# Two feed-forwards of a two-block network: a tile's two weight products as seven products of quarters (Strassen's scheme, Winograd's form)

## The chip, the cores and the metric

One core of one Trainium2 chip runs the whole program in one launch. The metric is the device time of that launch in microseconds (us); lower is better. The kernel before takes 3156.23 us, the median of 3 runs (3155.23 to 3160.46).

## What is computed

512 tokens of width 1024 go through two blocks of two layers each. Every layer is a mixer and a feed-forward behind an RMS norm. The change touches the feed-forwards of the second block alone:

```python
def swiglu(h, w_gate, w_up, w_down):
    return (jax.nn.silu(h @ w_gate) * (h @ w_up)) @ w_down

def second_block(x, ...):
    for l in range(DEPTH):              # DEPTH = 2
        ...
        h = rmsnorm(x, norm_ffn[l])
        x = x + swiglu(h, ffn_w_gate[l], ffn_w_up[l], ffn_w_down[l])
    return x
```

The gate and up weights are 1024 x 2816, the down weights 2816 x 1024, all float32.

## The kernel before

Activations are kept transposed: `h(k)`, k from 0 to 7, holds 128 channels by 512 tokens. Each float32 operand of TensorE is split into a rounded part and its rest (type fp32r), and each product takes three matmuls (`mm3`, line 481): high by high, low by high, high by low. The normed input lies in `xhi` and `xlo` (the list `X8`).

**Weights** (class `Weights`, line 287). A unit of up to 2048 columns is loaded by SyncE into one of three raw buffers (`wraw`), rounded by ScalarE into one of two `whi` (`round`), and VectorE takes the rest into `wlo` (`rest`). `round` of a unit waits until TensorE is done with the unit two before; a load waits for the `rest` of the unit three before. The programs of ScalarE and VectorE call `round` and `rest` with the unit that is being used, and do the next one.

**A feed-forward stage** (`ffn`, line 1095; stages `swiglu0` and `swiglu1`) has 22 tiles of 128 hidden channels. A tile's unit holds 128 columns of gate (named u) and 128 of up (named g) for all 8 input blocks. TensorE makes each with 8 x 3 matmuls of 512 tokens. ScalarE applies SiLU out of PSUM, VectorE multiplies by g, ScalarE rounds the product (`hid.hi`), VectorE takes the rest (`hid.lo`). The down product runs by groups of 8, 8 and 6 tiles, each group a group of tiles later than its ups; its units are 256 columns wide (two output blocks), and VectorE adds each output block from PSUM to `hT` (line 212).

**The start of a stage** (class `Fresh`, line 718). Tile 0 multiplies the not yet normed input (times the gain), so that TensorE doesn't wait for the norm; its results are scaled by `rs` afterwards. Meanwhile ScalarE makes `rs`, and VectorE and ScalarE make the normed, split input block by block; tile 1 takes the blocks as they come. In the midst of this (`midway`) comes the unit of tile 2.

**The end of a stage** (class `Carry`, line 680). After each output block is added to `hT`, ScalarE rounds it and squares it, VectorE takes its rest, and GpSimd (POOL) adds up the squares of blocks 1 to 6. The next stage's first tile needs the sum of squares before its third input block (`norm.sum`, at k == 2).

Apart from these sums of squares (78 additions of 128 x 512) GpSimd has almost no arithmetic. The engines wait for each other with semaphores that count; each engine's order is that in which its program is written.

## Time and profile before

| | before |
|---|---|
| median of 3 runs | 3156.23 us (3155.23 to 3160.46) |
| the profiled execution's own time | 3158.57 us |
| its span, first to last instruction | 3156.8 us |
| mean granted TensorE clock | 0.99 |
| TensorE matmul / weight load busy | 97% / 77% |
| VectorE / ScalarE / GpSimd busy | 50% / 37% / 4% |
| matmuls | 16544 |

The page of the profile gives each engine's busy time as a share of the span; a busy matmul row is not an engine at its peak, since matmuls overlap and their ends are modelled. So the time from one matmul's start to the next says more than the length of one. `swiglu0` runs from about 2003 to 2373 us, `swiglu1` from about 2784 to 3147 us.

### The profile page before, as it was taken

To read this page: it belongs to the slowest core of one execution; us is meant where nothing else is said; L and a number is where in the kernel's file an instruction comes from. 1 tells how busy PE (TensorE), PEld (TensorE's weight loads), DVE (VectorE), ACT (ScalarE), POOL (GpSimd) and SP (SyncE) were. 2 spreads that over 40 slices of the span, in tenths; PEclk is the share of its full clock that TensorE was granted. 3 is DMA by queue.
4 is the path that set the end of the run, shared out by engine and by line. 5 is a ranking of instruction groups with operands and counts; after the bars stand their busy time and mean duration, and the time that the engine had idled before them with its cause. 6 is when DMAs were issued, how large, how long until landed. Compare 5 with 4: busy or idle time off the path is not lost.

```text
span 3156.8 us, 38539 instructions
## 1 busy us (share of the span) xinstructions
PE 3047.3 (97%) x16544; PEld 2433.2 (77%) x16544; DVE 1571.3 (50%) x1919; ACT 1178.3 (37%) x1533; POOL 142.0 (4%) x154
## 2 busy tenths in 40 slices
PE   8999888999999999999999998999999999999999
PEld 6897676778887767778887775688888888788887
DVE  6444455655544765465444655533336454553333
ACT  5433332543322564443323545422224433342221
POOL 1010000100000100000001100000000000000000
PEclk9999999999999999999999999999999999999999
DMA  4362000223332311223332330233323222233331
GB/s 156 110 202 63 15 29 28 101 73 94 94 87 90 102 67 54 94 72 102 100 94 77 91 87 27 58 102 93 94 94 104 84 84 84 80 94 94 96 100 59
DMA packets 350490, 270.51 MB, mean 86 GB/s; under 512 B 28672, under 2 KB 331264, under 8 KB 350064
## 3 DMA queue, kind: packets, MB, share of 16 engines
q1 hardware_dynamic: 346384, 252.83, 26.8%
q0 software_dynamic: 3936, 15.22, 1.4%
q8 instruction: 130, 2.13, 0.3%
q14 instruction: 40, 0.33, 0.0%
HBM read 261.73 MB, written 6.29 MB: 85 GB/s over the span
## 4 chain that ended last, share of the span: by engine, by line
PE 86%; DVE 7%; ACT 5%; issue 1%; POOL 0%; DMA 0%; DVEq 0%; SPq 0%; ACTq 0%; POOLq 0%
PE ps L189 85%; ACT arena L203 2%; ACT whi L206 1%; DVE arena L212 1%; DVE arena L220 1%; DVE wlo L212 1%; DVE hT L212 1%; PE ps L192 1%; DVE xlo L220 1%; ACT L203 0%; DVE sml L229 0%; POOL arena L212 0%; DVE xlo L212 0%; ACT arena L206 0%; DVE split L212 0%
## 5 line engine op out<-in xcount | busy, mean ns | idle before, releaser
L189 PE MATMUL ps<-xhi,whi 128*128 128x512 f32 (+2 forms) x2176 | 866.1, 398 | 17.1 <-DVE xlo L212 5.6
L189 PE MATMUL ps<-split,whi 128*128 128x512 f32 (+2 forms) x2640 | 832.7, 392 | 22.2 <-DVE split L212 11.3
L189 PE MATMUL ps<-xlo,whi 128*128 128x512 f32 (+2 forms) x2176 | 849.5, 390 | 0.0
L189 PE MATMUL ps<-xhi,wlo 128*128 128x512 f32 (+2 forms) x2176 | 849.4, 390 | 0.0
L212 DVE TENSOR_TENSOR wlo<-wraw,whi 128x2048 fp32r<-128x2048 f32 (+4 forms) x258 | 550.6, 2137 | 498.9 <-ACT whi L206 498.8
L189 PEld LDWEIGHTS ps<-split,whi 128*128 128x128 f32 (+1 forms) x2640 | 490.5, 189 | 153.5 <-issue 30.2
L206 ACT ACTIVATE whi<-wraw 128x2048 fp32r<-128x2048 f32 (+4 forms) x258 | 456.1, 1771 | 362.0 <-PE ps L189 352.0
L189 PE MATMUL ps<-split,wlo 128*128 128x512 f32 (+2 forms) x1320 | 510.0, 386 | 0.0
L189 PEld LDWEIGHTS ps<-xhi,whi 128*128 128x128 f32 (+2 forms) x2176 | 408.3, 188 | 122.2 <-issue 15.0
L189 PEld LDWEIGHTS ps<-xhi,wlo 128*128 128x128 f32 (+2 forms) x2176 | 408.5, 188 | 88.0 <-issue 5.1
L189 PEld LDWEIGHTS ps<-xlo,whi 128*128 128x128 f32 (+2 forms) x2176 | 408.2, 188 | 88.3
L189 PE MATMUL ps<-arena 64*64 64x64 f32 (+8 forms) x4118 | 297.5, 262 | 24.6 <-ACT arena L203 9.9
L212 DVE TENSOR_TENSOR hT<-hT,ps 128x512 f32<-128x512 f32 x216 | 148.3, 686 | 322.7 <-PE ps L189 317.7
L206 ACT ACTIVATE arena<-ps 128x512 f32<-128x512 f32 (+2 forms) x262 | 144.4, 563 | 401.0 <-PE ps L189 311.7
L189 PEld LDWEIGHTS ps<-arena 64*64 64x64 f32 (+4 forms) x4118 | 213.2, 145 | 103.6 <-issue 54.0
L189 PEld LDWEIGHTS ps<-split,wlo 128*128 128x128 f32 (+1 forms) x1320 | 249.6, 189 | 53.9 <-issue 4.0
L212 DVE TENSOR_TENSOR arena<-arena,ps 128x512 f32<-128x512 f32 (+5 forms) x160 | 103.6, 647 | 368.0 <-PE ps L189 359.1
L206 ACT ACTIVATE split<-arena 128x512 fp32r<-128x512 f32 (+1 forms) x161 | 98.3, 615 | 430.0 <-DVE arena L212 421.0
L212 POOL TENSOR_TENSOR arena<-arena 128x512 f32<-128x512 f32 x78 | 106.8, 1373 | 2437.6 <-ACT arena L203 2436.7
L203 ACT ACTIVATE arena<-ps 128x512 f32<-128x512 f32 (+4 forms) x133 | 76.8, 584 | 262.7 <-PE ps L189 253.4
L203 ACT ACTIVATE arena<-arena 128x512 f32<-128x512 f32 (+4 forms) x154 | 93.4, 622 | 160.2 <-DVE arena L220 123.0
L212 DVE TENSOR_TENSOR split<-arena,split 128x512 fp32r<-128x512 f32 (+1 forms) x161 | 107.0, 670 | 80.6 <-ACT split L206 78.4
(115 smaller groups left out, 1924.3 us busy)
## 6 DMA issues: line engine op xcount, KB each, us to landing
wraw<-in_ffn_w_up SPq DMA_DIRECT2D x128, 512.0 KB, 5.2
wraw<-in_ffn_w_down SPq DMA_DIRECT2D x32, 1024.0 KB, 5.1
wraw<-in_odd_w_in SPq DMA_DIRECT2D x24, 1024.0 KB, 5.2
wraw<-in_ffn_w_gate SPq DMA_DIRECT2D x44, 512.0 KB, 4.0
wraw<-in_xattn_wkv SPq DMA_DIRECT2D x16, 1024.0 KB, 5.4
wraw<-in_xattn_wq SPq DMA_DIRECT2D x8, 1024.0 KB, 5.3
wraw<-in_xattn_wo SPq DMA_DIRECT2D x8, 1024.0 KB, 5.3
wraw<-in_cd_w_in SPq DMA_DIRECT2D x8, 1024.0 KB, 5.4
```

The lines of the kernel that those rows point to most:

```text
L189: return self.e.matmul(out, lhsT, rhs, start=start, stop=stop, skip_group_check=True)
L192: return self.e.transpose(out, in_, ident)
L203: return self.e.activation(out, in_, f, bias=bias, scale=scale, accum_out=acc)
L206: return self.e.activation(out, in_, ACT.Copy, scale=scale)
L212: return self.e.tensor_tensor(out, a, b, op)
L220: return self.e.scalar_tensor_tensor(out=out, in0=a, scalar=s, in1=b, op0=op0, op1=op1)
```

## The change

The stages `swiglu0` and `swiglu1` are made by a new function, `folded`. Tiles 0 to 2 are computed as before. From tile 3 on, a tile's weights are four quarters (A11, A12 are gate, A21, A22 are up; the second figure is the half of the input channels), the input is four quarters as well (B11 to B22, by halves of channels and of tokens), and both outputs come from seven products of quarters instead of eight. A product has 4 x 3 matmuls of 256 tokens.

- GpSimd makes four sums of weight quarters per tile (S1, S2, S4, and S3 in the place of A21 in the raw buffer). ScalarE rounds, and VectorE takes the rest of, 1536 columns more per tile; ScalarE waits for all four sums before it rounds the unit.
- VectorE makes four sums of input quarters (T1 to T4) once per stage, 1024 elements per partition each, and their rests; ScalarE rounds them.
- Bank a takes P1; ScalarE copies it out, and P6 and P7 are added up in the same bank, with a copy between. Bank c takes P5, and P3 on top. VectorE adds four halves of 256 tokens from PSUM to ScalarE's copies. SiLU then reads SBUF. A tile is multiplied, rounded and split in the next tile's turn (`finish(n - 1)`).
- The down groups are 3, 3, 3, 3, 3, 3 and 4 tiles; their units are 512 columns wide (4 output blocks), 14 units in place of 12, 56 additions to `hT` per stage in place of 24. In the last group the first unit runs over all 4 blocks at once, input tile by input tile (`by_tiles`).
- `FreshKept` keeps the normed input in full for T1 to T4.

The core of the diff:

```diff
+            if n in self.folded:
+                sums, hi, _, maker, tile = self.folded[n]
+                act.wait_ge(maker.of("sums", tile))
+                act.copy(final[1], final[0]).then_inc(*self.made_hi.up("quarters", n))
+                act.copy(hi, sums).then_inc(*self.made_hi.up(n))
+            else:
+                act.copy(final[1], final[0]).then_inc(*self.made_hi.up(n))
...
-            dve.wait_ge(self.made_hi.of(n))
+            dve.wait_ge(self.made_hi.of("quarters", n) if n in self.folded else self.made_hi.of(n))
             *first, final = self.halves(n)
             for raw, hi, lo in first:
                 dve.tt(lo, raw, hi.bitcast(F32), ALU.subtract)
-            dve.tt(final[2], final[0], final[1].bitcast(F32), ALU.subtract).then_inc(*self.made_lo.up(n))
+            if n in self.folded:
+                dve.tt(final[2], final[0], final[1].bitcast(F32), ALU.subtract)
+                sums, hi, lo, _, _ = self.folded[n]
+                dve.wait_ge(self.made_hi.of(n))
+                dve.tt(lo, sums, hi.bitcast(F32), ALU.subtract).then_inc(*self.made_lo.up(n))
+            else:
+                dve.tt(final[2], final[0], final[1].bitcast(F32), ALU.subtract).then_inc(*self.made_lo.up(n))
...
+        def folded(stage, w_u, w_g, w_down, ends, prev, nxt):
+            S = Stage(stage, sem)
+            nt, H = 22, 256
...
+            FIRST = 3
...
+            def group_of(n):
+                return min(n // 3, 6)
+            groups = [[n for n in range(nt) if group_of(n) == i] for i in range(7)]
...
+            def order():
+                for i, g in enumerate(groups):
+                    for n in g[0:3]:
+                        yield "up", n
+                    if i:
+                        yield "down", i - 1
+                yield "up", 21
+                yield "down", 6
...
+            def fold(n):
+                m = W.number[W.stage, ("up", n)]
+                W.folded[m] = (sums[m % 2], *extra(m % NSPL), S.G, n)
+                return m
+            def tensor(pe):
+                def product(b, u, e, a, x, first, *event, unit=None):
+                    for k in range(4):
+                        if a in ("s1", "s2", "s4"):
+                            i = ("s1", "s2", "s4").index(a)
+                            hi, lo = (t[:, i * T + k * P:i * T + k * P + P] for t in e)
+                        else:
+                            kk, c = {"a11": (k, 0), "a12": (4 + k, 0), "s3": (k, P), "a22": (4 + k, P)}[a]
+                            hi, lo = u.hi[:, kk, c:c + P], u.lo[:, kk, c:c + P]
+                        s = operand(x, k)
+                        pe.mm(b[:, 0:H], hi, s.hi, first and k == 0, False)
+                        pe.mm(b[:, 0:H], lo, s.hi, False, False)
+                        i_ = pe.mm(b[:, 0:H], hi, s.lo, False, k == 3)
+                    i_.then_inc(*up(S.P, *event, unit=unit))
+                def seven(n):
+                    u = W.take(("up", n), *unit(n))
+                    e = extra(fold(n) % NSPL)
+                    a, b, c, d = (ps.take(name, n) for name in "abcd")
+                    pe.wait_ge(W.ready(("up", n)), ps.empty("a", n), norm.made(7))
+                    product(a, u, e, "a11", "b11", True, "p1", n)
+                    pe.wait_ge(ps.empty("b", n))
+                    product(b, u, e, "a12", "b21", True, "p2", n)
+                    pe.wait_ge(ps.empty("c", n), S.V.of("t1"))
+                    product(c, u, e, "s1", "t1", True, "p5", n)
+                    pe.wait_ge(ps.empty("d", n), S.V.of("t4"))
+                    product(d, u, e, "a22", "t4", True, "p4", n)
+                    pe.wait_ge(S.A.of("p1", n), S.V.of("t2"))
+                    product(a, u, e, "s2", "t2", False, "u2", n)
+                    pe.wait_ge(S.A.of("p5", n))
+                    product(c, u, e, "s4", "b22", False, "c12", n)
+                    pe.wait_ge(S.A.of("u2", n), S.V.of("t3"))
+                    product(a, u, e, "s3", "t3", False, "u3", n, unit=("up", n))
...
+                        g = groups[n]
+                        for _ in add_tensor(pe, S, downs[n], [hid[k % 6] if k < 18 else hid[k - 18] for k in g],
+                                            [P] * len(g), lambda k: S.V.of("hid_lo", g[k]), by_tiles=n == 6):
...
+            def vector(dve):
...
+                    if n >= FIRST:
+                        finish(n - 1)
+                        for name, dst, half in (("b", y, slice(0, H)), ("c", y, slice(H, T)), ("d", g, slice(0, H)),
+                                                ("a", g, slice(H, T))):
+                            made = {"b": "p2", "c": "c12", "d": "p4", "a": "u3"}[name]
+                            kept_ = {"b": "p1", "c": "u2", "d": "u3", "a": "p5"}[name]
+                            dve.wait_ge(S.P.of(made, n), S.A.of(kept_, n))
+                            dve.tt(dst[:, half], dst[:, half], ps.ap(name, n)[:, 0:H], ALU.add).then_inc(
+                                *up(S.V, name, n, frees=(name, n)))
+                        dve.wait_ge(S.A.of("silu", n), S.V.own())
+                        dve.tt(y, y, g, ALU.mult).then_inc(*up(S.V, "hid", n))
+                        return
...
+                def finish(n):
+                    d = place(n)
+                    dve.wait_ge(S.A.of("hid_hi", n), S.V.own())
+                    dve.tt(d.lo, tb[n % 2], d.hi.bitcast(F32), ALU.subtract).then_inc(*up(S.V, "hid_lo", n))
+                dve.wait_ge(S.V.own())
+                dve.tt(tq["t1"][0], B12, B11, ALU.subtract).then_inc(*up(S.V, "t1", "sum"))
+                dve.wait_ge(S.V.own())
+                dve.tt(tq["t2"][0], B22, tq["t1"][0], ALU.subtract).then_inc(*up(S.V, "t2", "sum"))
+                dve.wait_ge(S.V.own())
+                dve.tt(tq["t4"][0], B21, tq["t2"][0], ALU.subtract).then_inc(*up(S.V, "t4", "sum"))
+                for what, n in order():
+                    if what == "up":
+                        up_tile(n)
+                        if n == 0:
+                            dve.wait_ge(S.V.own())
+                            dve.tt(tq["t3"][0], B22, B12, ALU.subtract).then_inc(*up(S.V, "t3", "sum"))
+                            low("t1")
+                            low("t2")
+                            low("t4")
+                        if n == 1:
+                            low("t3")
+                    else:
+                        if n == 6:
...
+                        for name, _, _, blocks in downs[n]:
+                            W.rest(dve, name)
+                            for key, m in blocks:
+                                d = h(key[-1])
+                                dve.wait_ge(S.P.of(*key), S.V.own())
+                                dve.tt(d, d, ps.ap(*key), ALU.add).then_inc(*up(S.V, "h", *key, frees=key))
+                                if n == 6 and carry and key[-1]:
+                                    carry.vector(dve, key[-1] - 1)
+                        if n == 6 and carry:
+                            carry.vector(dve, 7)
+            def scalar(act):
+                W.round(act, ("up", 0))
+                act.wait_ge(*ends())
+                norm.scalar(act, lambda: W.round(act, ("up", 1)))
...
+                    if n >= FIRST:
+                        for name, bank, dst, half in (("p1", "a", y, slice(0, H)), ("p5", "c", g, slice(H, T)),
+                                                      ("u2", "a", y, slice(H, T)), ("u3", "a", g, slice(0, H))):
+                            if name == "p5":
+                                finish(n - 1)
+                            if name == "u3":
+                                act.wait_ge(S.V.of("c", n))
+                                act.act(y, y, ACT.Silu).then_inc(*up(S.A, "silu", n))
+                            act.wait_ge(S.P.of(name, n), S.V.of("hid_lo", n - 2))
+                            act.copy(dst[:, half], ps.ap(bank, n)[:, 0:H]).then_inc(*up(S.A, name, n))
+                        return
...
+                for name in ("t1", "t2", "t4"):
+                    high(name)
...
+            def gpsimd(pool):
+                pool.wait_ge(*ends())
+                for n in range(FIRST, nt):
+                    m = W.number.get((W.stage, ("up", n)), 0)
+                    raw = W.raw[m % NRAW].rearrange("p (k n) -> p k n", k=8)
+                    A11, A12, A21, A22 = raw[:, 0:4, 0:P], raw[:, 4:8, 0:P], raw[:, 0:4, P:H], raw[:, 4:8, P:H]
+                    s1, s2, s4 = (sums[m % 2][:, i * T:(i + 1) * T].rearrange("p (k n) -> p k n", k=4) for i in range(3))
+                    pool.wait_ge(W.landed[m % NRAW].of(m), W.made_lo.of(m - 2))
+                    pool.tt(s1, A21, A22, ALU.add).then_inc(*up(S.G))
+                    pool.wait_ge(S.G.own())
+                    pool.tt(s2, s1, A11, ALU.subtract).then_inc(*up(S.G))
+                    pool.tt(A21, A11, A21, ALU.subtract).then_inc(*up(S.G))
+                    pool.wait_ge(S.G.own())
+                    pool.tt(s4, A12, s2, ALU.subtract).then_inc(*up(S.G, "sums", n))
...
-        then(lambda S: ffn("swiglu0", 0, 2816, D["ffn_w_gate_2"][0], D["ffn_w_up_2"][0],
-                           D["ffn_w_down_2"][0], False, S.ends, S.carry, lambda S: Carry(S, "norm_mix_2", 1)))
+        then(lambda S: folded("swiglu0", D["ffn_w_gate_2"][0], D["ffn_w_up_2"][0], D["ffn_w_down_2"][0],
+                              S.ends, S.carry, lambda S: Carry(S, "norm_mix_2", 1)))
         then(lambda S: odd(S.ends, S.carry, ("norm_ffn_2", 1)))
-        then(lambda S: ffn("swiglu1", 1, 2816, D["ffn_w_gate_2"][1], D["ffn_w_up_2"][1],
-                           D["ffn_w_down_2"][1], False, S.ends, S.carry, None))
+        then(lambda S: folded("swiglu1", D["ffn_w_gate_2"][1], D["ffn_w_up_2"][1], D["ffn_w_down_2"][1],
+                              S.ends, S.carry, None))
```

Two places of the new order. **VectorE at the start of `swiglu0`**, from the last two normed blocks' rests on (`xlo`), before the change:

```order
L212 TENSOR_TENSOR xlo<-arena,xhi 128x512 [waits swiglu0_done_vector,swiglu0_done_scalar]
L212 TENSOR_TENSOR arena<-ps2,arena 128x512 [waits swiglu0_done_tensor]
L212 TENSOR_TENSOR arena<-arena 128x512 [waits swiglu0_done_scalar]
L212 TENSOR_TENSOR arena<-arena,ps3 128x512 [waits swiglu0_done_vector,swiglu0_done_tensor]
L212 TENSOR_TENSOR split_51<-arena,split_51 128x512 [waits swiglu0_done_vector,swiglu0_done_scalar]
L212 TENSOR_TENSOR arena<-arena,ps6 128x512 [waits swiglu0_done_vector,swiglu0_done_tensor,swiglu0_done_scalar]
L212 TENSOR_TENSOR split_51<-arena,split_51 128x512 [waits swiglu0_done_vector,swiglu0_done_scalar]
L212 TENSOR_TENSOR wlo1<-wraw0,whi1 128x2048 [waits weights_hi]
```

and with the change (`split_51` is the arena in its rounded type; the rows of 1024 are T1, T2, T4, then T3, then the rests):

```order
L212 TENSOR_TENSOR arena<-arena 128x1024 [waits swiglu0_done_vector] x3
L212 TENSOR_TENSOR arena<-ps2,arena 128x512 [waits swiglu0_done_tensor]
L212 TENSOR_TENSOR arena<-arena 128x512 [waits swiglu0_done_scalar]
L212 TENSOR_TENSOR arena<-arena,ps3 128x512 [waits swiglu0_done_vector,swiglu0_done_tensor]
L212 TENSOR_TENSOR split_51<-arena,split_51 128x512 [waits swiglu0_done_vector,swiglu0_done_scalar]
L212 TENSOR_TENSOR arena<-arena 128x1024 [waits swiglu0_done_vector]
L212 TENSOR_TENSOR split_51<-arena,split_51 128x1024 x3
L212 TENSOR_TENSOR arena<-arena,ps6 128x512 [waits swiglu0_done_vector,swiglu0_done_tensor,swiglu0_done_scalar]
L212 TENSOR_TENSOR split_51<-arena,split_51 128x512 [waits swiglu0_done_vector,swiglu0_done_scalar]
L212 TENSOR_TENSOR split_51<-arena,split_51 128x1024
L212 TENSOR_TENSOR wlo1<-wraw0,whi1 128x2048 [waits weights_hi]
L212 TENSOR_TENSOR split_51<-arena,split_51 128x1536 [waits weights_hi]
```

Eight instructions of 1024 elements now stand between the normed input and the rest of tile 3's unit (`wlo1<-wraw0,whi1`), which itself has a second piece.

**ScalarE in a folded tile** (tile 4 of `swiglu0`), with the change; before, these were a rounding of 2048, a SiLU and a rounding of 512:

```order
L206 ACTIVATE whi1<-wraw2 128x2048 [waits swiglu0_done_gpsimd,weights_landed2]
L206 ACTIVATE split_51<-arena 128x1536
L206 ACTIVATE arena<-ps5 128x256 [waits swiglu0_done_tensor]
L206 ACTIVATE split_51<-arena 128x512 [waits swiglu0_done_vector]
L206 ACTIVATE arena<-ps7 128x256 [waits swiglu0_done_tensor]
L206 ACTIVATE arena<-ps5 128x256 [waits swiglu0_done_tensor]
L203 ACTIVATE arena<-arena 128x512 [waits swiglu0_done_vector]
```

The copy of P1 out of bank a (the first from `ps5`) now stands behind both roundings of the next unit and a wait for GpSimd.

## Rows read from the trace of the kernel before

**Rows 1.** The page: busy time by engine; the chain by engine.

```profile
PE 3047.3 (97%) x16544; PEld 2433.2 (77%) x16544; DVE 1571.3 (50%) x1919; ACT 1178.3 (37%) x1533; POOL 142.0 (4%) x154
PE 86%; DVE 7%; ACT 5%; issue 1%; POOL 0%; DMA 0%; DVEq 0%; SPq 0%; ACTq 0%; POOLq 0%
```

**Rows 2.** Windows: stretch, us, busy (count) of PE, PEld, DVE, ACT, POOL, clock.

```profile
2050.00:2180.00 130.00, 130.00 (x575) 107.63 (x575) 44.07 (x36) 36.17 (x36) 0.00 (x0) 1.00 0.34 97
160.00:216.00 56.00, 56.00 (x473) 56.00 (x474) 22.92 (x10) 23.54 (x28) 10.29 (x19) 1.00 0.74 230
...
2760.00:2764.00 4.00, 3.75 (x10) 2.98 (x11) 3.09 (x3) 1.04 (x2) 0.00 (x0) 0.57 0.00 0
```

**Rows 3.** Timeline of PE at 1763 us; 21 starts apart.

```profile
1763.37 0.28 PE L189 MATMUL ps<-wlo,xhi 128*128 128x256 f32 x1
...
1765.88 0.28 PE L189 MATMUL ps<-wlo,xhi 128*128 128x256 f32 x1
```

**Rows 4.** Groups by line and form: count, busy us, mean ns, idle.

```profile
L212 DVE TENSOR_TENSOR wlo<-wraw,whi 128x2048 fp32r<-128x2048 f32 x218 | 500.4, 2295 | 464.5 <-ACT whi L206 464.4
L212 DVE TENSOR_TENSOR wlo<-wraw,whi 128x1536 fp32r<-128x1536 f32 x10 | 17.6, 1758 | 11.1 <-ACT whi L206 11.1
L212 DVE TENSOR_TENSOR wlo<-wraw,whi 128x1024 fp32r<-128x1024 f32 x12 | 14.7, 1223 | 11.1 <-ACT whi L206 11.1
L212 DVE TENSOR_TENSOR arena<-arena,ps 128x256 f32<-128x256 f32 x7 | 2.9, 421 | 0.9 <-PE ps L189 0.6
...
L206 ACT ACTIVATE whi<-wraw 128x2048 fp32r<-128x2048 f32 x218 | 415.4, 1906 | 266.7 <-PE ps L189 256.7 <-DVE hT L212 10.0
L206 ACT ACTIVATE split<-arena 128x512 fp32r<-128x512 f32 x147 | 92.0, 631 | 426.8 <-DVE arena L212 418.3 <-DVE arena L220 8.5
L206 ACT ACTIVATE arena<-ps 128x256 f32<-128x256 f32 x40 | 15.3, 383 | 55.6 <-PE ps L189 38.4 <-PE ps L192 11.1 <-DMA kv_scratch<-arena 5.9
L206 ACT ACTIVATE whi<-wraw 128x1536 fp32r<-128x1536 f32 x10 | 14.8, 1483 | 51.8 <-PE ps L189 51.8
L206 ACT ACTIVATE whi<-wraw 128x1024 fp32r<-128x1024 f32 x12 | 12.6, 1048 | 5.9 <-PE ps L189 5.9
L203 ACT ACT_TABLE_LOAD x36 | 46.2, 1283 | 3.8 <-PE ps L189 3.2
```

**Rows 5.** Timeline of the start of swiglu0, DVE: start, us.

```profile
2011.38 2.29 DVE L212 TENSOR_TENSOR wlo<-wraw,whi 128x2048 fp32r<-128x2048 f32 x1 [0.79 <-ACT whi L206]
...
2023.37 2.29 DVE L212 TENSOR_TENSOR wlo<-wraw,whi 128x2048 fp32r<-128x2048 f32 x1 [2.33 <-ACT whi L206]
...
2029.01 1.48 DVE L212 TENSOR_TENSOR xlo<-arena,xhi 128x512 fp32r<-128x512 f32 x2
...
2037.99 2.29 DVE L212 TENSOR_TENSOR wlo<-wraw,whi 128x2048 fp32r<-128x2048 f32 x1 [1.11 <-ACT whi L206]
2043.75 0.69 DVE L212 TENSOR_TENSOR arena<-arena,ps 128x512 f32<-128x512 f32 x1 [3.46 <-PE ps L189]
```

**Rows 6.** Timeline of DVE and POOL at 555 us, at the end of a mixer.

```profile
555.67 1.79 DVE L220 SCALAR_TENSOR_TENSOR xlo<-hT,par,xhi 128x512 fp32r<-128x512 f32 x1
...
559.61 0.69 DVE L212 TENSOR_TENSOR hT<-hT,ps 128x512 f32<-128x512 f32 x1
...
555.62 1.29 POOL L212 TENSOR_TENSOR arena<-arena 128x512 f32<-128x512 f32 x1 [309.65 <-ACT arena L203]
...
559.62 1.30 POOL L212 TENSOR_TENSOR arena<-arena 128x512 f32<-128x512 f32 x1 [0.66 <-ACT arena L203]
```

**Rows 7.** Timeline of the start of swiglu1, DVE.

```profile
2802.77 1.48 DVE L212 TENSOR_TENSOR xlo<-arena,xhi 128x512 fp32r<-128x512 f32 x2
...
2817.52 0.69 DVE L212 TENSOR_TENSOR arena<-arena,ps 128x512 f32<-128x512 f32 x1 [3.48 <-PE ps L189]
```

**Rows 8.** Timeline of the end of swiglu0: ACT's last square, PE's sum of squares.

```profile
2374.96 0.62 ACT L203 ACTIVATE arena<-hT 128x512 f32<-128x512 f32 x1
...
2376.14 1.88 PE L189 MATMUL ps<-arena,ones 128*128 128x512 f32 x4
```

152 lines of the change are left out of this document (151 added, 1 removed).

## The prediction

> **What bounds the kernel now.** I read the page first: TensorE's matmuls are busy for 97% of the span and make up 86% of the chain that ended last, no other engine over 7% [rows 1]. So the chain is TensorE's stream, and what counts is the time from one matmul's start to the next, and every stop of that stream. The windows give the first: in swiglu0, 575 matmuls of 512 columns in 130 us, 0.226 us each; and for 256 columns, where weights or moving data lie in the arena, 473 in 56 us, 0.118 us each [rows 2]. With `xhi` and `xlo` the timeline has 21 starts of 256 columns in 2.51 us, 0.120 us each [rows 3]. All at a granted clock of 1.00, the level of 2.4 GHz. Halving the columns thus costs a little over half. The idle column of the groups says the same from the other side: VectorE waits for ScalarE's rounding and ScalarE's rounding for TensorE [rows 4].
>
> **What the seven products save.** A tile before: 48 x 0.226 = 10.85 us. A folded tile: 84 matmuls of 256; 36 of them (P1, P2, P3) move `xhi` or `xlo`, 36 x 0.120 = 4.30, and 48 lie in the arena, 48 x 0.118 = 5.68: 9.98 us. Saved 0.87 us a tile, on 19 tiles in 2 stages: **-33 us**. The down products keep their 528 matmuls of 512 per stage and cost the same.
> The Trainium skill (TensorE: Matmul & The Clock Gate, Back-to-back issue gap) says that in a stream with a weight load before each matmul the spacing is 81 ns at 128 columns and 131 ns at 512. A straight line between gives 98 ns at 256, an estimate from that page: 84 x 98 ns is 8.2 us against 48 x 131 ns, 6.3 us, so by that rule each folded tile would lose 1.9 us. The trace has 226 and 118 to 120 ns, so it speaks against the rule here.
>
> **In the middle of a stage.** I lay out one folded tile, 0 being TensorE's first matmul of it, with [rows 4]. ScalarE: copy of the last product of the tile before 0.38 (done 0.6), unit rounded 1.91 (2.5), sums rounded 1.48 (3.9), copy of P1 0.38 (4.3). TensorE wants that copy before P6, after four products, at 5.7: 1.4 us to spare. Copies of P5 (5.3, wanted at 7.2) and of bank a again (7.7, wanted at 8.6) have room too. VectorE: two halves from PSUM 0.42 each, the product 0.69 [rows 6] (2.2), rest of the unit 2.3 (4.8), rest of the sums 1.76 (6.5), wanted at 10. GpSimd: 4 x 1.30 and two waits, 5.4 us a tile, started when the rests of the unit two before are made; a whole tile of room. Per group of three tiles TensorE needs 3 x 9.98 + 72 x 0.23 = 46.5 us, VectorE about 30, ScalarE 21, GpSimd 16. The 32 more additions to `hT` per stage (0.69 us each) are in VectorE's 30 and cost nothing as long as that cover holds; without it they would cost 22 us a stage. So I put the middle at **0**. Weight loads move no more bytes and start at the same rests: 0.
>
> **The start of a stage** is where I expect the loss. Before, VectorE ends the norm at 2030.49 and has tile 3's unit split at 2040.28, 3.2 us ahead of TensorE, which ends tile 2 at about 2043.5 [rows 5]. Now between these two stand, one behind the other, because VectorE and ScalarE hand to each other: T1, T2, T4, 3 x (1.22 + 0.11 for the wait) to 34.5; u of tile 0 scaled, 35.2; ScalarE rounds T4 only to 35.6, then loads its table 1.28 and SiLU 0.63, 37.6; two products 39.1; rounding 0.63 and rest 0.69, 40.5; T3 41.8; three rests of 1.22, 45.5; tile 1's product, rounding, rest 47.6; T3's rest 48.8; ScalarE ends the second piece of tile 3's unit at 50.2; VectorE 2.29 and 1.76: **2052.8**. TensorE is free at 2043.5: a stop of 9.3 us.
> GpSimd adds to this. At 555 us a two-input VectorE instruction of 0.75 us takes 1.79 and ends 0.55 us behind the GpSimd addition that runs beside it (555.62 + 1.29 to 557.46), while the addition to `hT` from PSUM at 559.61 takes its 0.69 beside one at 559.62 [rows 6]. So a GpSimd addition and a VectorE instruction with both inputs in SBUF exclude each other, in turns, about 1.15 us for each of GpSimd's. The sums of tile 3 may start when tile 1's unit is split (2011.38 + 2.29), against the first normed blocks, which delays `midway` by 1.3 us (VectorE waits 2.33 us ahead of it now) [rows 5]; those of tile 4 when tile 2's unit is split (2025.6 before, now about 2027), against the last three blocks: 4 x 1.15 = 4.6, less 0.5 where VectorE waits anyway. I come to a delay of 5.4 us: stop 14.7. Swiglu1 has no slack at the first block; the same walk from 2804.25 with a delay of 6.6, against tile 2's end at 2817.4 [rows 7], gives 15.8. Together **+30.5 us**; without GpSimd's part +18.6, the lower end; twice its part +43, the upper.
> After such a stop TensorE runs at the lower level: granted 0.57, 10 matmuls in 4 us, after 5 us in which it had done little [rows 2]. At 0.226 each 18 would have gone: 1.4 to 1.8 us lost, I take 1.4 each: **+2.8 us** (0 to 3.6).
>
> **The end of swiglu0.** Before, the last square ends at 2375.58 and the sum of squares starts without a wait at 2376.14 [rows 8]. Now four blocks end together, and the next stage's first unit is rounded only after their four squares, in VectorE's order ahead of block 4's addition. From the end of the first unit: GpSimd's square sums and VectorE's rests take turns, squares of blocks 0 to 3 done 5.1, unit rounded 7.0, split 9.3, then blocks 4 to 7 at about 2.0 us each (the spacing of GpSimd's additions at 555 us, (559.62 - 555.62) / 2 with one left out [rows 6]), last square 17.3. TensorE has the second unit until 48 x 0.23 = 11.1 and two input blocks of the next until 13.8: **+3.5 us** (1 to 6). Swiglu1 ends without this.
>
> **Sum.** -33.1 + 30.5 + 2.8 + 3.5 = +3.7 us on the profiled execution's own 3158.57 us: 3162.3. That execution is 2.3 us above the median of the runs, and I put the difference on the median: 3156.2 + 3.7 = **3160 us**. About 0.2% (6.3 us) is what a measurement of this kernel can tell from no change.
>
> **Rivals.**
> - *GpSimd's sums don't cost VectorE anything*: the start loses 18.6 + 2.8, the end of swiglu0 about 2. For it: VectorE idles before `midway`, and the port may go to VectorE more often than in turns. Against: rows 6. Time 3156.2 - 33.1 + 23.4 = 3146.5. Chance 0.22.
> - *The stops of the start are hidden altogether* (tile 3 need not wait, since something in my walk overlaps): -33 + 3.5, 3127. Against: the order is written out, each step waits for the one before. Chance 0.05.
> - *Slower: TensorE stops in every folded tile for the copy of P1.* ScalarE's queue puts it behind two roundings and a wait for GpSimd's four sums. It decides from 5.7 us after the tile's start; I have 4.3. Half a microsecond past it costs 38 x 0.5 = 19: 3179. For it: both engines ahead are slowed in turns with GpSimd. Against: GpSimd has a tile of room. Chance 0.15.
> - *The weight loads bind*: 84 loads for 48, if 256 columns can't cover one. At the page's spacing the loss of 1.9 us a tile would be 73 us; from rows, if the matmuls went at the 0.19 us that a load is busy (107.63 us over 575 loads [rows 2]), 84 x 0.19 = 16 us a tile, far slower. Against: 0.118 to 0.120 us is seen over hundreds. Chance 0.03.
>
> **How the numbers follow.** The forecast, 3154 to 3166 by the bounds of its terms (1 ns in the spacing of a short matmul is 3.2 us), has 0.55. Faster by over 0.2% (under 3149.9): most of the first rival, the second, a little of the forecast: 0.26. Slower by over 0.2% (above 3162.5): a third of the forecast, the third and fourth rival: 0.36. Same: 0.38. The range, 3143 to 3178, takes in the first rival and the near part of the third and leaves out the rest.
>
> **What would show it.** In the profile after: PE windows over folded tiles at 0.119 us a matmul, about 10.0 us a tile; a stop of TensorE before tile 3 of 9 to 10 us in each stage, with small ones for `xlo` in tile 1, the end of the stop set by VectorE's second piece (128x1536, `split<-arena,split`); a clock of about 0.5 behind it; two-input VectorE instructions lengthened beside GpSimd's in the first 40 us of a stage. Stops in later tiles, a spacing away from 0.119, or a tile 3 that starts without a stop would make the prediction wrong.

## The result, and the profile after

| | before | after |
|---|---|---|
| median, run side by side | 3158.50 us (3155.23 to 3163.01, 16 runs) | 3164.43 us (3162.93 to 3168.11, 16 runs) |
| ratio | | 1.002, 95% interval 1.0013 to 1.0027 |
| span of the profiled execution | 3156.8 us | 3164.3 us |
| mean granted TensorE clock | 0.990 | 0.985 |
| matmuls | 16544 | 17912 |

The change makes the kernel about 6 us slower. The forecast was 3160.0 us, slower by 3.7, in a range of 3143 to 3178. About half of the 4.4 us between 3160.0 and 3164.43 is the base: the forecast started from 3156.2 us for the kernel before, which measured 3158.50 beside the change.

The page of the profile after, busy time by engine and the chain that ended last, to be held against [rows 1]:

```profile
PE 3028.6 (96%) x17912; PEld 2480.7 (78%) x17912; DVE 1780.7 (56%) x2193; ACT 1290.1 (41%) x1735; POOL 353.8 (11%) x306
PE 83%; DVE 9%; ACT 5%; issue 2%; POOL 0%; DMA 0%; DVEq 0%; SPq 0%; ACTq 0%; POOLq 0%
```

TensorE is busy for 19 us less although the kernel is slower: the share of VectorE in the chain grew from 7% to 9%. That is work saved on TensorE and time lost in front of it.

Three marks cut the profiled execution into stretches: the first `ones` matmul of swiglu0, of the stage after it, and of swiglu1, then the first output transpose.

| stretch | before | after | difference |
|---|---|---|---|
| up to swiglu0's first sum | 2009.69 | 2010.25 | +0.6 |
| swiglu0 and its end | 366.45 | 369.68 | +3.2 |
| the stage between | 408.79 | 410.33 | +1.5 |
| swiglu1 | 363.24 | 365.39 | +2.2 |

The first stretch is the same code in all kernels; over the eleven profiled executions of this study it lies between 2007.1 and 2012.9 us, so single spans differ by some us for no reason of the change. The stage between, also the same code, lies between 407.3 and 412.7 us. The two changed stages are the better measure: swiglu1 takes 365.39 us here, and 364.24 and 365.18 us in e4 and e7, which differ from the change only at the end of a stage.

**Folded tiles.** The window view of swiglu0, of three folded tiles and of the down group behind them; then that of before, six tiles and down products. The columns are as in [rows 2].

```profile
2106.87:2137.02 30.15, 30.15 (x253) 30.15 (x252) 18.11 (x21) 15.14 (x22) 8.57 (x7) 1.00 0.39 116
2137.02:2153.82 16.80, 16.80 (x75) 13.52 (x73) 11.71 (x13) 5.06 (x4) 7.15 (x6) 1.00 0.29 72
```

```profile
2229.72:2295.02 65.30, 65.30 (x290) 54.07 (x289) 21.34 (x17) 17.71 (x17) 0.00 (x0) 1.00 0.31 97
2184.93:2229.72 44.79, 44.79 (x193) 36.04 (x192) 15.35 (x13) 8.19 (x5) 0.00 (x0) 1.00 0.34 94
```

The ends of these windows are starts of matmuls, and a window also counts the matmuls that still run at its start. A folded tile takes 30.15 / 3 = 10.05 us (252 matmuls, 0.1197 us each), an unfolded one 65.30 / 6 = 10.88 us (288, 0.2267 each): 0.83 us saved a tile. The down products take 0.2333 us a matmul in both (72 in 16.80, 192 in 44.79), and there are 528 of them a stage in both. The engines are also as laid out: VectorE 18.1 + 11.7 = 29.8 us of a group of 46.95, ScalarE 20.2, GpSimd 15.7.

**The start of swiglu0.** PE's timeline at tile 1 and at tile 3, the rows that waited (in brackets the idle time ahead and what ended it), then the chain of waits from the norm's end on (start, us, what):

```profile
2029.81 0.50 PE L189 MATMUL ps<-xhi,whi 128*128 128x512 f32 x1 [2.28 <-DVE xlo L212]
2033.17 0.50 PE L189 MATMUL ps<-xhi,whi 128*128 128x512 f32 x1 [1.71 <-DVE xlo L212]
2035.47 0.50 PE L189 MATMUL ps<-xhi,whi 128*128 128x512 f32 x1 [0.64 <-DVE xlo L212]
...
2057.93 0.58 PE L189 MATMUL ps<-xhi,whi 128*128 128x256 f32 x1 [8.58 <-DVE split L212]
```

```profile
2036.23 1.24 DVE arena L212
...
2037.49 1.24 DVE arena L212
...
2038.75 1.24 DVE arena L212
...
2041.09 1.28 ACT L203
...
2047.19 3.42 DVE split L212 x3
...
2052.11 1.83 DVE split L212 x2
2053.94 1.41 DVE wlo L212
...
2056.12 1.76 DVE split L212
2057.93 4.21 PE ps L189 x18
```

This is the row of hand-overs of the prediction: T1, T2, T4, ScalarE's table, T3 and three rests, tile 1's rest and T3's rest, tile 3's unit and its second piece. TensorE stops three times in tile 1 and once before tile 3, and not again until the end of the stage: the long chain entry from 2057.93 lasts 303 us (below).

VectorE and GpSimd in tile 1, side by side (one timeline, VectorE's rows first):

```profile
2028.00 1.75 DVE L212 TENSOR_TENSOR xlo<-arena,xhi 128x512 fp32r<-128x512 f32 x1
2029.68 1.77 DVE L220 SCALAR_TENSOR_TENSOR arena<-hT,par,arena 128x512 f32<-128x512 f32 x1
...
2027.56 1.64 POOL L212 TENSOR_TENSOR arena<-wraw 128x512 f32<-128x512 f32 x1 [6.76 <-DVE wlo L212]
2029.28 1.62 POOL L212 TENSOR_TENSOR arena<-arena,wraw 128x512 f32<-128x512 f32 x1
```

A rest of a block takes 1.75 us where it took 0.74 before ([rows 5]: two in 1.48). Four additions of GpSimd lengthen four to five instructions of VectorE by about 1 us each.

**The clock.** Windows behind the stop before tile 3, and behind the stop at the end of swiglu0:

```profile
2058.00:2062.00 4.00, 4.00 (x19) 4.00 (x20) 4.00 (x3) 1.81 (x3) 3.91 (x2) 0.50 0.60 197
2380.00:2384.00 4.00, 4.00 (x8) 1.99 (x9) 3.04 (x2) 2.05 (x2) 1.61 (x3) 0.62 0.31 93
```

In the first the granted clock is 0.50, the level of 1.2 GHz: 19 matmuls of 256 columns in 4 us where 33 go at full clock. In the second the mean is 0.62, a stretch at 1.2 GHz and the rest at 2.4. In swiglu1 the first stop of tile 1 already brings it (starts 0.43 us apart from 2810.02 to 2811.73 and from 2813.52 to 2816.51).

**The end of swiglu0.** The chain of waits, and PE's timeline at the sum of squares, which answers to [rows 8]:

```profile
2057.93 303.04 PE ps L189 x2067
...
2368.09 1.81 ACT whi L206
2369.96 2.17 issue
```

```profile
2379.93 3.50 PE L189 MATMUL ps<-arena,ones 128*128 128x512 f32 x4 [2.93 <-ACT arena L203]
```

### The profile page after: what moved, and what is told of

Read it like the earlier page. It is cut to its first block, busy times and chain, and to the rows that moved or that the text cites. A ratio compares the mean times of both kernels' runs of the same rounds, so it can differ in the third digit from the quotient of the medians.

```text
span 3164.3 us, 42011 instructions
## 1 busy us (share of the span) xinstructions
PE 3028.6 (96%) x17912; PEld 2480.7 (78%) x17912; DVE 1780.7 (56%) x2193; ACT 1290.1 (41%) x1735; POOL 353.8 (11%) x306
## 4 chain that ended last, share of the span: by engine, by line
PE 83%; DVE 9%; ACT 5%; issue 2%; POOL 0%; DMA 0%; DVEq 0%; SPq 0%; ACTq 0%; POOLq 0%
PE ps L189 82%; ACT arena L203 2%; DVE arena L220 2%; DVE arena L212 2%; ACT whi L206 1%; DVE hT L212 1%; DVE wlo L212 1%; PE ps L192 1%; DVE xlo L220 1%; DVE split L212 1%; ACT L203 0%; DVE sml L229 0%; POOL arena L212 0%; DVE xlo L212 0%; ACT split L206 0%
## 5 line engine op out<-in xcount | busy, mean ns | idle before, releaser
L189 PE MATMUL ps<-split,whi 128*128 128x512 f32 (+1 forms) x3248 | 953.2, 371 | 22.1 <-DVE split L212 11.0
L189 PEld LDWEIGHTS ps<-split,whi 128*128 128x128 f32 x3248 | 587.4, 189 | 153.0 <-issue 30.8
L189 PE MATMUL ps<-xhi,wlo 128*128 128x512 f32 (+2 forms) x1872 | 703.2, 376 | 0.0
L189 PE MATMUL ps<-xlo,whi 128*128 128x512 f32 (+2 forms) x1872 | 703.0, 376 | 0.0
L189 PEld LDWEIGHTS ps<-xhi,whi 128*128 128x128 f32 (+1 forms) x1872 | 355.8, 190 | 126.4 <-DVE xlo L212 19.0
L189 PEld LDWEIGHTS ps<-xhi,wlo 128*128 128x128 f32 (+1 forms) x1872 | 356.0, 190 | 65.9 <-issue 5.7
L189 PEld LDWEIGHTS ps<-xlo,whi 128*128 128x128 f32 (+1 forms) x1872 | 355.7, 190 | 65.1
L206 ACT ACTIVATE split<-arena 128x512 fp32r<-128x512 f32 (+3 forms) x207 | 162.7, 790 | 219.9 <-DVE arena L212 211.0
L212 DVE TENSOR_TENSOR split<-arena,split 128x512 fp32r<-128x512 f32 (+3 forms) x207 | 184.8, 909 | 54.0 <-ACT split L206 51.8
L189 PE MATMUL ps<-split 128*128 128x256 f32 (+3 forms) x1200 | 168.5, 292 | 0.0
```

Source lines behind the costliest of these rows:

```text
L189: return self.e.matmul(out, lhsT, rhs, start=start, stop=stop, skip_group_check=True)
L206: return self.e.activation(out, in_, ACT.Copy, scale=scale)
L212: return self.e.tensor_tensor(out, a, b, op)
```

## Experiments

Each kernel was run beside the kernel before, and its ratio is to that. In the diffs "-" is the change unless another kernel is named. Stage differences are from the marks above.

### e1: without T1 to T4

```diff
-                    pe.wait_ge(ps.empty("c", n), S.V.of("t1"))
+                    pe.wait_ge(ps.empty("c", n))
...
-                dve.tt(tq["t1"][0], B12, B11, ALU.subtract).then_inc(*up(S.V, "t1", "sum"))
...
-                for name in ("t1", "t2", "t4"):
-                    high(name)
```

and likewise for T2 to T4; the four products that need them take plain quarters of the input.

> The changed kernel without the four sums of input quarters: VectorE makes no T1 to T4 and no rests of them, ScalarE rounds none, and the products that took them take plain quarters of the normed input instead, so the two feed-forwards' values are not the reference's. My theory (tile 3 of each stage waits for a chain of steps between VectorE and ScalarE, of which these sums, roundings and rests are some 9 us): tile 3's unit is split at about 2048 us in swiglu0, before TensorE has ended tile 2 at about 2049, so the stops of 9.0 and 8.2 us before tile 3 are gone, and the slow clock behind them with it; the stops in tile 1 stay, 5.8 and 6 us. Time about 3164.4 - 19 = 3145, 3142 to 3149. Rival (the stop comes from GpSimd's sums of tile 3 arriving late): the stop stays whole and the time within 2 us of 3164.

Measured: 3139.86 us (3137.17 to 3141.92), ratio 0.9941 (0.9929 to 0.9954). Swiglu0 is 11.9 us shorter than in the change, swiglu1 12.8. The stop before tile 3 is gone; the stops in tile 1 are all there:

```profile
2027.13 0.50 PE L189 MATMUL ps<-xhi,whi 128*128 128x512 f32 x1 [2.30 <-DVE xlo L212]
2030.50 0.50 PE L189 MATMUL ps<-xhi,whi 128*128 128x512 f32 x1 [1.71 <-DVE xlo L212]
2032.79 0.50 PE L189 MATMUL ps<-xhi,whi 128*128 128x512 f32 x1 [0.64 <-DVE xlo L212]
```

So tile 3's stop hangs on the T work, and tile 1's does not. The time is 5 us below the 3145 expected, and below the range. Of these, 3.0 are the slow clock behind the two stops: 2.0 and 2.8 us (below), where the expectation had 1.8 for both. Another 1.5 are the slow clock behind the stop at the end of swiglu0, which is as long here (2.99 us of waiting) but is followed by no slow clock; nothing shows that the T work has a part in that.

### e2: folding from tile 5

```diff
-            FIRST = 3
+            FIRST = 5
```

> The changed kernel with FIRST = 5: tiles 3 and 4 are computed as before, the first sums of weight quarters are those of tile 5 and start only when tile 3's unit is split. Theory (GpSimd's additions and VectorE's two-input instructions exclude each other, which costs 5.4 and 6.6 us at the starts): tile 1 runs without its stops of 2.7, 2.1 and 1.0 us, VectorE's instructions of 0.75 us keep their length there, the stop before tile 3 stays at 7 to 8 us. Gain 6 + 7 us at the starts, against 4 tiles x 0.87 = 3.5 us that are no longer folded: about 3154.5, 3152 to 3158. Rival (the start is lost to the T sums alone): no gain at the start, 3164.4 + 3.5 = 3168.

Measured: 3154.15 us (3153.01 to 3156.07), ratio 0.9989 (0.998 to 0.9998), as the theory had it. The first GpSimd sums now come after the norm, and the stops of tile 1 are gone (0.2 us left, as in before). But tile 3, unfolded and in no need of T1 to T4, still waits for its unit, behind them in VectorE's order:

```profile
2048.30 0.79 PE L189 MATMUL ps<-xhi,whi 128*128 128x512 f32 x1 [6.70 <-DVE wlo L212]
```

The kernel is 10 us faster than the change, and by about 3 us faster than before, with four tiles fewer folded: what a tile saves is less than where its preparation stands.

### e3: the kernel before, with GpSimd's sums at the stage starts

Eight additions of 128x512 in swiglu0 and swiglu1 each, four when tile 1's unit is split and four when tile 2's is, on memory that nothing else uses, and once a stage a clearing of that memory ahead of them:

```diff
...
+                    for n in (3, 4):
+                        m = W.number.get((W.stage, ("up", n)), 0)
+                        pool.wait_ge(W.made_lo.of(m - 2), S.G.own())
+                        pool.tt(s1, s3, s4, ALU.add).then_inc(*up(S.G))
...
```

> The kernel before, with nothing but eight additions of 128x512 (and one clearing of their operands) put on GpSimd at the start of swiglu0 and of swiglu1, in the order and behind the same waits for the split units as the sums of tiles 3 and 4, on data of their own that nobody reads. It computes what the kernel before does. Theory (exclusion): the stops in tile 1 appear as in the changed kernel, VectorE's two-input instructions beside the additions lengthen to 1.2 to 1.9 us, and tile 3 has no stop, since VectorE's slack ahead of it shifts with TensorE: +5.4 and +6.6 us, about 3158.5 + 12 = 3170, 3167 to 3172. Rival (no exclusion, the stops in tile 1 have another cause): 3158.5 within 2 us.

Measured: 3168.70 us (3168.02 to 3171.37), ratio 1.0035 (1.0021 to 1.0048), as the theory had it; swiglu0 +5.5, swiglu1 +6.9 against before. There is no stop before tile 3. No engine waits for these sums, and none of the data is shared. The timeline, VectorE's rows and then GpSimd's four:

```profile
2026.96 1.77 DVE L212 TENSOR_TENSOR xlo<-arena,xhi 128x512 fp32r<-128x512 f32 x1
2028.77 1.66 DVE L220 SCALAR_TENSOR_TENSOR arena<-hT,par,arena 128x512 f32<-128x512 f32 x1
2030.34 1.76 DVE L212 TENSOR_TENSOR xlo<-arena,xhi 128x512 fp32r<-128x512 f32 x1
...
2026.46 6.78 POOL L212 TENSOR_TENSOR arena<-arena 128x512 f32<-128x512 f32 x4 [6.90 <-DVE wlo L212]
```

This is the cost by itself of GpSimd's additions beside VectorE's instructions with two inputs in SBUF. The stops in tile 1, less those of before, are 4.0 us in swiglu0 and 4.3 in swiglu1, from start to start. The rest is slow clock. In swiglu1 it is 2.5 us behind the first of these stops (granted 0.50 at 2807 to 2811). In swiglu0 it is 1.5 us more than in before, in tile 0 and so ahead of the stops (starts 0.43 us apart up to 2015.01), behind the stop at the first sum of squares that before has too; whether the additions have a part in that is not shown. The clearing, 1.80 us at 2009.91, lengthens nothing: VectorE's rest of 2048 columns beside it takes its usual 2.29 us.

### e4: the last down group in units of 256 columns

```diff
+                bw = 256 if i == 6 else 512
...
```

and the unit's columns and blocks follow `bw`.

> The changed kernel with the last down group (tiles 18 to 21) in units of 256 columns, two output blocks each, as in the kernel before. Theory (the next stage's first unit is rounded behind the squares of four blocks and stands in VectorE's order ahead of block 4's addition): the stop of 3.3 us before the sum of squares at the end of swiglu0 goes, and the slow sum of squares and first matmuls behind it (1.6 us) too; the end of swiglu1 does not change. 3164.4 - 4.9 = 3159.5, 3158.5 to 3162. Rival (the stop is set by the time that blocks 4 to 7 come out of TensorE): no change, 3164.4.

Measured: 3163.11 us (3160.63 to 3166.69), ratio 1.0018 (1.0009 to 1.0027): 1.3 us under the change, whose ratio of 1.0020 lies in e4's interval, and above the 3162 expected at most. The stop ahead of the sum of squares is gone, but there is another, ahead of the next stage's first unit:

```profile
2372.20 0.40 PE L189 MATMUL ps<-split,whi 128*128 128x512 f32 x1
2374.49 0.69 PE L189 MATMUL ps<-xhi,whi 128*128 128x512 f32 x1 [1.90 <-DVE wlo L212]
```

`round` and `rest` may run one unit ahead, since there are two slots. With small units one unit ahead is half the time, so the next stage's first unit is rounded after block 5's square and not after block 3's.

### e5: T1 to T4 moved behind tiles 1 to 3, folding from tile 5

Against e2:

```diff
-                dve.tt(tq["t1"][0], B12, B11, ALU.subtract).then_inc(*up(S.V, "t1", "sum"))
...
                         finish(n)
+                        if n == 1:
+                            dve.tt(tq["t1"][0], B12, B11, ALU.subtract).then_inc(*up(S.V, "t1", "sum"))
...
+                        if n == 3:
+                            for name in ("t1", "t2", "t4", "t3"):
+                                low(name)
```

and on ScalarE the four roundings behind tile 2 (`if n == 2`).

> The change with tiles 3 and 4 left unfolded (folding starts at tile 5) and the sums T1 to T4, their roundings and their rests moved from ahead of tile 0 and behind tile 0 to behind tiles 1, 2 and 3. Theory (the loss is where the T sums stand, in a chain of waits between VectorE and ScalarE ahead of tile 3's unit, and GpSimd's sums beside the norm): both stops before tile 3 are gone (7.1 us each in the run that only starts folding at tile 5) and the stops in tile 1 too (0.6 left at most). Then 17 folded tiles x 0.87 us x 2 = -29.6 us, +4.9 us for the end of swiglu0 as in the change (stop and slow clock after it): 3158 - 24.7 = 3133 us, 3130 to 3141. Rival (VectorE has too much to do in the first tiles, wherever its T work stands): a stop of several us comes before tile 4 or 5, 3147 or more.

Measured: 3137.75 us (3136.78 to 3138.86), ratio 0.9939 (0.9927 to 0.9952), inside the expected range, 4.8 us above the 3133 of the theory. Swiglu0 is 10.7 us shorter than before, swiglu1 13.7. By the measured tile, 17 x 0.83 = 14.1 us a stage less 0.3 at tile 4 (starts 0.53 us apart at 2056.24) is 13.8 in swiglu1; in swiglu0 3.1 us of it are lost at the stage's end, where the stop is as in the change but no slow clock follows. In the chain of waits TensorE runs from tile 1 on; T4 and T3 still stand ahead of tile 4's unit, which comes 0.3 us late:

```profile
2029.12 16.65 PE ps L189 x72
...
2048.13 3.39 DVE arena L212 x2
...
2052.50 1.91 ACT whi L206
2054.43 2.30 DVE wlo L212
2056.78 43.29 PE ps L189 x248
```

GpSimd's sums now stand beside VectorE's T4 and T3, which take 3.45 us where T1 and T2 took 2.48, at a place with room:

```profile
2038.80 2.48 DVE L212 TENSOR_TENSOR arena<-arena 128x1024 f32<-128x1024 f32 x2
...
2048.05 3.45 DVE L212 TENSOR_TENSOR arena<-arena 128x1024 f32<-128x1024 f32 x2
```

### e6 and e7: the end of swiglu0, once more

In the last down group VectorE takes the rest of the next stage's first unit behind the additions of blocks 4 and 5, not ahead of block 4; e7 is the change with this move, e6 is e5 with it.

```diff
-                            W.rest(dve, name)
+                            late = n == 6 and name[-1] == 512
+                            if not late:
+                                W.rest(dve, name)
                             for key, m in blocks:
+                                if late and key[-1] == 6:
+                                    W.rest(dve, name)
```

> The kernel of the run before, and in the last down group VectorE's rest of the next stage's first unit placed behind the additions of blocks 4 and 5 instead of ahead of block 4. Theory (the end of swiglu0 costs because that rest and its wait for the rounding, 4.1 us, stand ahead of block 4's addition): the last square ends about 2.4 us sooner, the stop before the sum of squares falls from 3.3 to about 0.9 us, and with it most of the slow clock after it: 3 us below the run before, 3130 us, 3127 to 3139. Rival (the next unit, split late, is waited for in its place): no gain, or a loss of 1 to 2 us.

> The change with that one move alone (the rest of the next stage's first unit behind blocks 4 and 5). Theory: 3163.5 - 3 = 3160.5 us, 3159.5 to 3162, the stop before the sum of squares at 0.9 us. Rival (the wait moves to the next unit): 3163 or more.

Measured: e6 3137.59 us (3136.31 to 3139.86), ratio 0.9939 (0.9927 to 0.9952), the same as e5; e7 3162.89 us (3160.62 to 3166.18), ratio 1.0017 (1.0008 to 1.0026), 1.5 us under the change and above the 3162 expected at most. Theory and rival were each half right: the old stop went, and a new one came. From e7's timeline:

```profile
2377.70 0.48 PE L189 MATMUL ps<-xhi,whi 128*128 128x512 f32 x1 [0.87 <-DVE wlo L212]
...
2381.47 1.10 PE L189 MATMUL ps<-arena,ones 128*128 128x512 f32 x2 [0.78 <-ACT arena L203]
```

The wait for the sum of squares fell from 2.93 to 0.78 us, and 0.87 us came up ahead of the next unit, whose rest now runs beside GpSimd:

```profile
2374.17 3.38 DVE L212 TENSOR_TENSOR wlo<-wraw,whi 128x2048 fp32r<-128x2048 f32 x1
```

3.38 us for 2.29. Its swiglu0 and the stage after it are together 3.0 us shorter than in the change, but its first stretch is 2.6 us longer, and the medians, 1.5 us apart, don't tell a gain from none. Neither e4's move nor this one mends the end.

### e8: folding from tile 4, the T work one tile earlier than in e5

> The run with T1 to T4 late, with folding from tile 4 and the sums, roundings and rests of T1 to T4 each one tile earlier. One tile more is folded in each stage: -1.7 us. But GpSimd's first four sums now start when tile 2's unit is split, beside the norm's last blocks. Theory (they exclude VectorE's instructions with two inputs in SBUF there, about 1.15 us each): 2 to 4 us more of stops in tile 1 of each stage, in all 3137.8 - 1.7 + 4 to 8: 3140 to 3144 us. Rival (beside the norm GpSimd's sums cost little, the T sums' place is all): 3136 us.

```diff
-            FIRST = 5
+            FIRST = 4
...
-                        if n == 1:
+                        if n == 0:
                             dve.wait_ge(S.V.own())
                             dve.tt(tq["t1"][0], B12, B11, ALU.subtract).then_inc(*up(S.V, "t1", "sum"))
...
```

and likewise for T4, T3, the roundings and the rests. ("-" is e5.) Measured: 3153.91 us (3150.31 to 3157.81), ratio 0.9989 (0.998 to 0.9998), 16 us above e5 and 10 above the expected range. The stops in tile 1 are 4.1 us as the theory had it (four sums of GpSimd beside the norm's last blocks). Left out of the expectation was tile 3:

```profile
2039.56 4.73 ACT L206 ACTIVATE split<-arena 128x512 fp32r<-128x512 f32 x5 [3.62 <-DVE arena L212]
2044.19 1.90 ACT L206 ACTIVATE whi<-wraw 128x2048 fp32r<-128x2048 f32 x1
```

```profile
2048.47 0.50 PE L189 MATMUL ps<-xhi,whi 128*128 128x512 f32 x1 [3.29 <-DVE wlo L212]
...
2062.15 0.39 PE L189 MATMUL ps<-xhi,whi 128*128 128x256 f32 x1 [0.92 <-DVE split L212]
```

ScalarE's roundings of T1 to T4 stand one tile too early, ahead of tile 3's unit, and wait for VectorE's sums. One tile earlier saves 1.7 us by the tile folded, and in all it is 16 us slower. Two causes share that. GpSimd's four sums beside the norm cost 3.7 us more of stops in tile 1 of each stage than in e5. The T work, put in front of tile 3's unit, costs a stop of 3.5 us there in each stage, one of 1.1 and 1.4 us before tile 4, and about 3 us of slow clock (starts 0.43 us apart behind both of tile 3's stops).

### e9: the change, with GpSimd held until the norm's end

```diff
-                pool.wait_ge(*ends())
+                pool.wait_ge(*ends(), S.V.of("norm", "lo", 7))
```

> The change, with GpSimd held until the norm's last rest, so that its first sums no longer run beside the norm but beside T1 to T4 and tile 0's work. Theory (GpSimd's addition and VectorE's instruction with two inputs in SBUF take turns wherever they meet; what a norm loses is a delay of the one chain that ends at tile 3's unit): the stops in tile 1 (5.1 us) go, the stop before tile 3 grows by as much, 8.7 to about 13.5 us; time as the change, 3161 to 3166 us. Rival (the sums cost only where every block's waits meet them, in the norm): stop before tile 3 stays at 9 us or so, 3153 us.

Measured: 3162.38 us (3160.66 to 3165.98), ratio 1.0017 (1.0008 to 1.0026), as the theory had it. Tile 1 runs through, and the stop before tile 3 has grown from 8.58 to 12.56 us (about 13.5 expected). The timelines of PE, VectorE and GpSimd:

```profile
2056.95 0.58 PE L189 MATMUL ps<-xhi,whi 128*128 128x256 f32 x1 [12.56 <-DVE split L212]
```

```profile
2031.02 5.70 DVE L212 TENSOR_TENSOR arena<-arena 128x1024 f32<-128x1024 f32 x3
...
2031.33 2.07 POOL L212 TENSOR_TENSOR arena<-wraw 128x512 f32<-128x512 f32 x1 [21.35 <-DVE xlo L212]
2033.48 2.16 POOL L212 TENSOR_TENSOR arena<-arena,wraw 128x512 f32<-128x512 f32 x1
```

T1, T2 and T4 take 5.70 us in place of 3.75, and GpSimd's additions are lengthened as well, to 2.1 from 1.29. So a chain of waits pays for the exclusion wherever it meets it. e5 differs: there it meets work with room.

## Why the prediction was right

**What bounds the kernel.** Right: TensorE's stream, and stops of it.

**What the seven products save.** The mechanism was right, the size a little off: 0.87 us a tile was forecast, 0.83 measured, 38 x 0.83 = -31.5 in place of -33.1 us. An unfolded tile is 10.88 (10.85 forecast), a folded one 10.05 (9.98): its 84 matmuls are 0.1197 us apart, and the 0.118 read from the window at 160 us for those with both sides in the arena was too good: its 473 matmuls in 56 us take in some that began before it, and the starts in it are 0.119 apart.

By an estimate from the figures of the Trainium skill (TensorE: Matmul & The Clock Gate, Back-to-back issue gap) each folded tile would have lost 1.9 us. The trace of after, with 0.1197 and 0.2267 us from start to start, disagrees as that of before did.

**The middle of a stage at 0.** Right. No stop between tile 3 and the last group in either stage. In tile 4 of swiglu0 (TensorE from about 2070.0) ScalarE's copy of P1 runs at

```profile
2073.63 0.38 ACT L206 ACTIVATE arena<-ps 128x256 f32<-128x256 f32 x1
```

and so is done 4.0 us after the tile's start; 4.3 was forecast and 5.7 is when it decides. The third rival (a stop in every tile) was thus off by the 1.7 us that it needed.

**The start of a stage.** Right in kind, too high by a fifth. Stops in swiglu0: 5.1 us in tile 1 and 8.7 before tile 3, less 0.4 that before has too, 13.4 (14.7 forecast); in swiglu1 4.7 + 8.0 - 0.4 = 12.3 (15.8). The stop before tile 3 is thus a little under the 9 to 10 us that were to show it, and ends as said with VectorE's second piece. GpSimd's share, the stops in tile 1, was the more overrated: 4.7 and 4.3 us, where 5.4 and 6.6 were reckoned. That it is GpSimd's, which the first rival denied, was tested in three ways: e1 leaves these stops where they are, e3 makes them alone in the kernel before, at 4.0 and 4.3 us, and e9 moves them. That e3's stages are longer by 5.5 and 6.9 us, close to the 5.4 and 6.6, is chance: the slow clock in them was no part of those terms. The T chain, forecast at 9.3 and 9.2 us a stage, gave 11.9 and 12.8 when taken out (e1), more than its stop of 8.7 and 8.0: the slow clock behind the stop belongs to it, which makes 10.7 and 10.8. What the other 1.2 and 2.0 us are was not told apart.

**The slow clock** was the term mis-sized most. 1.4 us a stop was forecast, 2.8 in all, from a row of 512-column matmuls behind 5 us of little work. Behind the stops before tile 3 it cost 2.0 and 2.8 us (the first 252 matmuls of 256 columns took 32.14 and 32.97 us, later ones 30.15). In swiglu1 the first stop of tile 1 brought another 2.8 us, 13 starts 0.43 to 0.59 us apart. Together 7.6.

**The end of swiglu0.** Right: a stop of 3.1 us (3.5 forecast), with the cause named there. TensorE ends the first unit at 2362.9; from there the last square ends after 16.9 us, where 17.3 was reckoned, and TensorE has work for 13.9, where 13.8 was. The slow clock after it, another 1.5 us in the next stage, had no term. It does not come in every execution: e1 and e5 have the same stop without it. e4 and e7 show that the place of the rounded unit and the chain of squares are both tight: freeing the one stops the other.

**The sum** by what was measured: -31.5 + 25.7 + 7.6 + 4.6 = +6.4 us, against +6.9 by the marks and +5.9 by the medians. Forecast was +3.7. Two errors of opposite sign met: stops 4.8 too high, clock 6.3 too low with the 1.5 at the end counted in; the saving came out 1.6 smaller and the end's stop 0.4 smaller. So the mechanism was foreseen, but that the sum lies within 2.2 us of the measured difference is in part luck.

## What to carry to other kernels

A scheme that takes work off the bounding engine brings preparation with it, once a stage, and the place where this stands in the other engines' orders decides. Here 19 folded tiles a stage lose 6 us and 17 win 20. Two moves make that up: 10 us come from folding later, which takes GpSimd's sums out of the norm (e2), and 16 from the input sums standing behind tiles 1 to 3 and not ahead of tile 0 (e5 against e2). Before counting what a step saves, list what waits behind it on its engine, and give new work to GpSimd only where VectorE's two-input instructions beside it have room. A stop of TensorE is to be priced with the slow clock behind it, which in the profiled execution was a third as much again (9.1 us of slow clock to 28.8 of stops).

## What the hardware showed

- The exclusion of GpSimd and VectorE works both ways. An addition of 128x512 on GpSimd takes 1.29 us alone, 1.6 beside VectorE's instructions of 512 elements and 2.1 to 2.3 beside those of 1024 (e9), while VectorE's go from 0.74 to 1.75 us. The Trainium skill (SBUF — State Buffer, SBUF: two separate sides) says the same of the rule: a VectorE operation with two SBUF inputs and a GpSimd one that reads SBUF lock each other out for a whole instruction; the ends of the rows above agree: VectorE's instructions end at 2029.75 and 2031.45, each 0.55 us behind the GpSimd addition beside it, at 2029.20 and 2030.90. With 16 additions that no engine waits for, e3 is 11 to 12 us slower in all, slow clock included.
- The clock fell to 0.50 (1.2 GHz) behind a stop of 3.6 us in swiglu1's tile 1 (starts 3.80 us apart), and not behind the three stops of 0.8 to 2.4 us in swiglu0's tile 1: no start behind them was over 0.36 us from the one before. In e3, where the stop in swiglu1 was as long (3.47 us of waiting), the clock fell too:

```profile
2807.00:2811.00 4.00, 2.96 (x7) 1.85 (x7) 3.93 (x4) 0.63 (x1) 3.85 (x3) 0.50 0.89 243
```

- The length of a stop alone does not tell whether the slow clock follows. Behind the stop before the sum of squares at the end of swiglu0, 2.93 us of waiting, the change has 0.62 (above); behind the same stop in e5, 2.92 us, the clock stays at 1.00. What decides it was not tried.

```profile
2367.00:2371.00 4.00, 3.30 (x11) 2.13 (x12) 3.11 (x3) 3.60 (x4) 1.82 (x4) 1.00 0.14 24
```

- A matmul of 512 columns is 0.2267 us apart from the next in the gate and up products and 0.2333 in the down products, in before and after alike. Why was not tried.
- The stretch ahead of swiglu0, the same code in all kernels, varies by 5.8 us between profiled executions, and the stage between the two changed ones by 5.4, so differences of two or three us are read from the changed stages and not from spans. Where these us come from was not looked for.
